# Hybrid decoder step: the product of the end-weighted x and B as three rounded products in units 2 to 5 of each group

## What is computed

```python
a_cum = jnp.cumsum(dtg * A.reshape(g, e).astype(f32), axis=2)
xdt = xg * dtg[..., None]
...
y_diag = jnp.einsum('bcijg,bcijge,bcjgep->bcigep', cb, decay, xdt)
decay_to_end = jnp.exp(a_cum[:, :, -1:] - a_cum)
chunk_states = jnp.einsum('bcjgn,bcjge,bcjgep->bcgepn', Bg, decay_to_end, xdt)
...
def step(s, inp):
    st, dec = inp
    return s * dec[..., None, None] + st, s
...
y_off = jnp.einsum('bcign,bcgepn,bcige->bcigep', Cg, starts, jnp.exp(a_cum))
```

## Time and profile before

| | us |
|---|---|
| median of 3 runs | 959.5 (958.59 to 961.35) |
| the profiled execution | 960.14 |
| its span | 958.3 |
| PE busy | 938.4 |
| DVE busy | 558.9 |
| ACT busy | 476.9 |
| POOL busy | 323.7 |
| PE, L1619, 20 products (40 records) | 587 to 692 ns a record, first at 544.3, last at 920.0 |

### The profile page before, as it was taken

How to read it: one execution, slowest core, us unless ns; L and a number is a source line. 1 busy time by engine, 2 the same in 40 slices (tenths; PEclk the granted TensorE clock), 3 DMA queues, 4 the chain that set the end, 5 groups by cost and what they waited for, 6 DMA issues and landing times.

```text
span 958.3 us, 18425 instructions
## 1 busy us (share of the span) xinstructions
PE 938.4 (98%) x7252; PEld 872.3 (91%) x7252; DVE 558.9 (58%) x1428; ACT 476.9 (50%) x943; POOL 323.7 (34%) x257
## 2 busy tenths in 40 slices
PE   9999999999999999999999999999999999999898
PEld 8998899989998899988998889998899989998787
DVE  4234421444225332447688679865898568986782
ACT  6335613365234623267537575446562565626852
POOL 2442244224431343224724232622434223442500
PEclk9999999999999999999999999999999999999999
DMA  7522231342143221211334825247152572327303
GB/s 212 181 75 68 77 100 53 110 152 77 57 118 146 95 88 52 89 23 45 113 96 128 233 61 168 89 119 222 46 162 91 151 205 70 128 85 216 108 12 105
DMA packets 144614, 105.91 MB, mean 111 GB/s; under 512 B 10754, under 2 KB 135860, under 8 KB 144464
## 3 DMA queue, kind: packets, MB, share of 16 engines
q1 hardware_dynamic: 134536, 100.19, 34.5%
q10 hardware_dynamic: 9992, 4.54, 2.0%
HBM read 91.99 MB, written 16.79 MB: 114 GB/s over the span
## 4 chain that ended last, share of the span: by engine, by line
PE 87%; DVE 9%; issue 2%; ACT 1%; DMA 0%; POOL 0%; SPq 0%; DVEq 0%; ACTq 0%; POOLq 0%
PE pp L1285 22%; PE pp L1287 21%; PE pp L1286 21%; PE pS L1395 2%; PE pO L1619 2%; PE pO L1615 2%; PE pT_ L1605 2%; PE pO L1442 1%; PE pO L1441 1%; DVE s_in L2312 1%; PE pO L1566 1%; PE pS L1538 1%; PE pp L1337 1%; PE pS L1576 1%; PE pT_ L1417 1%
## 5 line engine op out<-in xcount | busy, mean ns | idle before, releaser
L706 POOL TENSOR_TENSOR w_lo_buf<-w_raw_buf,w_hi_buf 128x512 fp32r<-128x512 f32 x214 | 278.9, 1334 | 475.7 <-ACT w_hi_buf L782 298.1
L1285 PE MATMUL pp<-h_hi,w_hi_buf 128*128 128x280 f32 (+2 forms) x1248 | 378.8, 304 | 2.1 <-issue 1.6
L1287 PE MATMUL pp<-h_hi,w_lo_buf 128*128 128x280 f32 (+2 forms) x1248 | 363.2, 291 | 0.0
L1286 PE MATMUL pp<-h_lo,w_hi_buf 128*128 128x280 f32 (+2 forms) x1248 | 362.6, 291 | 0.0
L1285 PEld LDWEIGHTS pp<-h_hi,w_hi_buf 128*128 128x128 f32 x1248 | 235.2, 188 | 11.9 <-issue 10.1
L1286 PEld LDWEIGHTS pp<-h_lo,w_hi_buf 128*128 128x128 f32 x1248 | 235.3, 189 | 5.3 <-issue 4.8
L1287 PEld LDWEIGHTS pp<-h_hi,w_lo_buf 128*128 128x128 f32 x1248 | 235.5, 189 | 0.0
L782 ACT ACTIVATE w_hi_buf<-w_raw_buf 128x2048 fp32r<-128x2048 f32 (+1 forms) x55 | 104.1, 1892 | 48.3 <-DMA w_raw_buf<-in_w_ssm_in 24.7
L1805 DVE TENSOR_TENSOR x<-x,pp 128x272 f32<-128x272 f32 (+2 forms) x120 | 53.1, 442 | 81.9 <-PE pp L1287 81.2
L1285 PE MATMUL pp<-og_hi,w_hi_buf 128*128 128x280 f32 (+2 forms) x256 | 75.6, 295 | 3.1 <-DVE x L1805 2.0
L1287 PE MATMUL pp<-og_hi,w_lo_buf 128*128 128x280 f32 (+2 forms) x256 | 74.5, 291 | 0.0
(11 more groups left out here) (357 smaller groups left out, 1613.8 us busy)
## 6 DMA issues: line engine op xcount, KB each, us to landing
w_raw_buf<-in_w_attn_in SPq DMA_DIRECT2D x16, 1024.0 KB, 5.2
w_raw_buf<-in_w_ssm_in SPq DMA_DIRECT2D x16, 1024.0 KB, 5.9
w_raw_buf<-in_w_attn_out SPq DMA_DIRECT2D x8, 1024.0 KB, 5.3
s_in<-in_state_ssm SPq DMA_DIRECT2D x32, 256.0 KB, 3.8
out<-s_in SPq DMA_DIRECT2D x32, 256.0 KB, 3.8
w_raw_buf<-in_w_ssm_out SPq DMA_DIRECT2D x8, 1024.0 KB, 6.6
seg<-a_scratch SPq DMA_DIRECT2D x12, 512.0 KB, 5.3
w_raw_buf<-in_w_attn_in SPq DMA_DIRECT2D x8, 512.0 KB, 6.2
```

Source lines behind the costliest of these rows:

```text
L706: ins = pool.tensor_tensor(low_buf(n)[:, piece], raw[n % RAW_SLOTS][:, piece], high_buf(n)[:, piece].bitcast(F32), ALU.subtract)
L1285: pe.matmul(dst, hi[:, k, cols], a_hi[:, k, tk], start=(k == 0), stop=False)
L1286: pe.matmul(dst, hi[:, k, cols], a_lo[:, k, tk], start=False, stop=False)
L1287: mm = pe.matmul(dst, lo[:, k, cols], a_hi[:, k, tk], start=False, stop=(k == depth - 1))
```

## The change

In units 2 to 5 of each group, 16 in all, the product of `btok` and `xw` is made of three products of rounded halves. The high half of B is a rounding copy from PSUM by DVE, the low half a DVE subtraction that waits for it; both stand in `prepare`. The high half of `xw` is a copy by ACT (`high_xw`, after `start_decay(u)`), its low half a subtraction by DVE in place of `xw` (`low_xw`, last in iteration u). The first of the three products waits for `low_xw`. `xw_hi` lies where `cv0` is, `btok_lo` where `sT1` is. Unit 1 (16 tokens) keeps its float32 product. Unit 0 has none.

```diff
--- before.py
+++ after.py
@@ -311,6 +311,9 @@
         xw = at("xw", [P, 2, WIDTH])
         cbm = at("cbm", [P, 2, P])
         btok = at("btok", [P, 2, P])
+        btok_hi = at("btok_hi", [P, 2, P], F32R, offset=where["btok"])
+        xw_lo = at("xw_lo", [P, 2, WIDTH], F32R, offset=where["xw"])
+        xw_hi = at("xw_hi", [P, 2, WIDTH], F32R, offset=where["cv0"])
         state = at("state", [P, WIDTH])
         ec = [at(f"ec{i}", [P, HEADS, P]) for i in range(2)]
         s_in = [at(f"s_in{i}", [P, HEADS, P]) for i in range(DEC_B - 2)]
@@ -318,6 +321,7 @@
         s_in += [at(f"s_in{6 + i}", [P, HEADS, P], offset=where["seg2"] + 4 * WIDTH * i) for i in range(2)]
         sT = [at(f"sT{i}", [P, WIDTH]) for i in range(2)]
         sT += [at("sT2", [P, WIDTH], offset=where["xdt"] + 4 * WIDTH), at("sT3", [P, WIDTH], offset=where["xw"] + 4 * WIDTH)]
+        btok_lo = at("btok_lo", [P, 2, P], F32R, offset=where["sT1"])
         c_own = at("c_own", [P, DEC_B * SAMPLE])
 
         x_parts = at("x_parts", [STACK, WIDTH], F32R, offset=where["rb0"] + 32)
@@ -369,6 +373,7 @@
         w_hi, w_lo = sem("w_hi"), sem("w_lo")
         p_done, p_evac = sem("p_done"), sem("p_evac")
         par_tr, par_ready, ones_ready = sem("par_tr"), sem("par_ready"), sem("ones_ready")
+        xw_high, xw_low = sem("xw_high"), sem("xw_low")
         x_tr, x_ready, h_ready = sem("x_tr"), sem("x_ready"), sem("h_ready")
         high_x = sem("high_x")
         sqx_ready, ssx_done, rs_ready = sem("sqx_ready"), sem("ssx_done"), sem("rs_ready")
@@ -1135,6 +1140,12 @@
                     act.wait_ge(clamped, w + 1)
                     act.activation(e, e, ACT.Exp, scale=-1.0).then_inc(l_done, 1)
 
+                def high_xw(u):
+                    v = UNITS * g + u
+                    act.wait_ge(xw_done, v + 1)
+                    act.wait_ge(b_done, v - 1)
+                    act.activation(xw_hi[:, v % 2, :], xw[:, v % 2, :], ACT.Copy).then_inc(xw_high, 1)
+
                 def start_decay(u):
                     act.wait_ge(ec_in[u % 2], 32 * (2 * g + (u - 2) // 2 + 1))
                     act.activation(ec[u % 2][:, :, :], ec[u % 2][:, :, :], ACT.Exp).then_inc(ec_ready, 1)
@@ -1184,6 +1195,7 @@
                         if u == 5:
                             start_decay(4)
                         start_decay(u)
+                    high_xw(u)
                     if (g, u) == (GROUPS - 1, 2):
                         silu_z(z_order(s)[0:HEADS])
                         exp_tables()
@@ -1616,7 +1628,15 @@
                                   start=True, stop=True)
                 if u == 1:
                     pe.wait_ge(sT_ready, DEC_B * (g + 1))
-                pe.matmul(pO[:, 0, :], btok[0:n, v % 2, :], xw[0:n, v % 2, :], start=True, stop=True).then_inc(b_done, 1)
+                if c == 0:
+                    pe.matmul(pO[:, 0, :], btok[0:n, v % 2, :], xw[0:n, v % 2, :],
+                              start=True, stop=True).then_inc(b_done, 1)
+                    return
+                pe.wait_ge(xw_low, 4 * g + u - 1)
+                pe.matmul(pO[:, 0, :], btok_hi[:, v % 2, :], xw_hi[:, v % 2, :], start=True, stop=False)
+                pe.matmul(pO[:, 0, :], btok_hi[:, v % 2, :], xw_lo[:, v % 2, :], start=False, stop=False)
+                pe.matmul(pO[:, 0, :], btok_lo[:, v % 2, :], xw_hi[:, v % 2, :],
+                          start=False, stop=True).then_inc(b_done, 1)
 
             def sum_y(g, part):
                 tk = part_of(g, part)
@@ -2105,11 +2125,22 @@
                     return
                 if c:
                     dve.tensor_tensor(cbm[0:n, b, 0:n], pS[0:n, 0, 0:n], mask, ALU.mult)
-                dve.tensor_copy(btok[0:n, b, :], pS[0:n, 0, P:2 * P])
+                if c:
+                    link(dve.tensor_copy(btok_hi[:, b, :], pS[:, 0, P:2 * P]))
+                    dve.tensor_tensor(btok_lo[:, b, :], pS[:, 0, P:2 * P], btok_hi[:, b, :].bitcast(F32), ALU.subtract)
+                else:
+                    dve.tensor_copy(btok[0:n, b, :], pS[0:n, 0, P:2 * P])
                 dve.tensor_tensor(heads(xdt[0:n, b, :], n), heads(pS[0:n, 1, :], n),
                                   per_head(tok2[0:n, 0, c, hs], n), ALU.mult)
                 dve.tensor_tensor(heads(xw[0:n, b, :], n), heads(pS[0:n, 1, :], n),
                                   per_head(wend[0:n, c, hs], n), ALU.mult).then_inc(xw_done, 1)
+
+            def low_xw(g, u):
+
+                v = UNITS * g + u
+                dve.wait_ge(xw_high, 4 * g + u - 1)
+                dve.tensor_tensor(xw_lo[:, v % 2, :], xw[:, v % 2, :], xw_hi[:, v % 2, :].bitcast(F32),
+                                  ALU.subtract).then_inc(xw_low, 1)
 
             def mix(g, u):
 
@@ -2331,6 +2362,7 @@
                         conv_in(g + 1, 0, u - 4)
                     if u > 2:
                         add_skip(g, u - 1)
+                    low_xw(g, u)
                 if g + 1 < GROUPS:
                     gate_y(g, 0)
                     conv_in(g + 1, 1, 0)
```

## The result

| | before | with the change |
|---|---|---|
| median, us | 959.4 (4 runs, 958.6 to 961.4) | 971.3 (4 runs, 969.7 to 972.3) |
| profiled execution, us | 960.1 | 969.7 |
| its span, us | 958.3 | 967.9 |

The ratio is 1.0126, 95% interval 1.0113 to 1.0140: slower by 11.9 us. Forecast were 7.2 slower, 966.7, with a range up to 970.5. The direction and the places of PE's waits were right, the size was not, and the result lies above the range.

What follows compares the result with a forecast made beforehand. PE was taken to bound the kernel. Groups 0 to 2 add 3.9 us and group 3 adds 3.3, +7.2 in sum: 967.3 for the profiled execution, 966.7 as median; range with the rivals 962.5 to 970.5.

Steps and rivals of the forecast that it cites:

- What bounds the kernel: PE, busy 938.4 of 958.3 us with 87% of the last chain; no gap in group 0's 6.76 us period.
- the ring: Groups 0 to 2: low_xw, PE's products, POOL's decay, DVE's row and back, 7.06 us a unit against PE's 6.58.
- DVE's uncovered row: Groups 0 to 2: DVE's gapless work from the state's addition to the next unit's first operation, 4.23 us, 5.06 in unit 4.
- The failed step: Unit 4, groups 0 to 2: low_xw takes 0.69 to 1.20 us beside POOL's split, making PE +1.2 to +1.7 us late.
- The 1.3 taken for a group: Loss chosen for each of groups 0 to 2 from a range of +1.0 to +1.5 us; three groups +3.9.
- PE's saving: Units 2 to 5: three rounded products take 0.68 us where one float32 product took 0.86; 16 x 0.18 = 2.9.
- Behind unit 5: End of groups 0 to 2: no cost added; unit 5's low_xw is in time and PE gets 0.18 us back.
- its own upper value: Groups 0 to 2: 1.5 us per group, which would hold if GpSimd contention slows low_xw as it did L2158.
- Group 3: ACT's late xw_hi delays mix(3) by 1.35 us; later waits make sum_y +3.3 us late.
- The one that cost more: Rival: products save nothing or low_xw takes 1.20 us everywhere in the nine binding products; +9 to +12 us, chance 0.14.
- Faster: Rival: all 16 waits fall inside earlier work and only PE's saving of 2.9 us is left; 956.6 us, chance 0.05.
- half covered: Rival: low_xw takes 0.3 us less, so the waits shrink; +4.5, 964 us; chance 0.09 for landing within 0.3%.

Runs made afterwards that it cites:

- e8: The change with POOL's splits of the weights in pieces of 256 columns instead of 512: 965.4 us, 6.9 above the kernel before.
- e5: The kernel before with DVE writing B and xw rounded and PE multiplying the high halves three times, no low halves: 956.8 us against 958.5.
- e4: The change's added DVE and ACT operations, but PE keeps the float32 product and waits for none of them: 964.4 us, 5.2 above the kernel before.
- e2: The change with ACT's xw_hi copy of unit 2 in group 3 moved behind the SiLU and table loads: 967.7 us, 8.6 above the kernel before.
- e7: As e4, without ACT's copy; DVE subtracts xw from itself and waits for no one: 962.1 us, 3.6 above the kernel before.
- e1: The change with low_xw moved right behind mix, ahead of the evacuation and add_skip: 969.5 us, 10.4 above the kernel before.
- e3: The change with POOL's weight split in groups 0 to 2 moved behind the state's decay of unit 4: 967.6 us, 8.4 above the kernel before.
- e9: The kernel before with POOL's splits in pieces of 256 columns instead of 512: 958.5 us against 958.4.
- e11: The change in groups 0 to 2 alone, group 3 computing as before: 967.1 us, 8.7 above the kernel before.
- e12: The kernel before with POOL pieces of 256 columns and the three rounded products only in unit 2 of groups 0 to 2: 958.0 us against 959.1.
- e10: The change with POOL pieces of 256 columns and ACT's copy of unit 2 in group 3 behind the SiLU: 963.6 us, 5.2 above the kernel before.

## Why the prediction was wrong

The trace puts the loss of groups 0 to 2 into few places. How much later than before the projection behind each product starts, counted from the start of part_a of unit 2 (from the starts of L1286 and L1298):

| us | unit 2 | unit 3 | unit 4 | unit 5 | whole group |
|---|---|---|---|---|---|
| forecast | -0.18 | +0.12 | +1.2 to +1.7 | +1.0 to +1.5 | +1.3 |
| group 0 | -0.16 | +0.23 | +2.49 | +2.32 | +2.57 |
| groups 1 and 2 | -0.16 | +0.23 | +2.50 | +2.32 | +2.28, +2.33 |

- *What bounds the kernel, and the ring.* Right. PE waits for `low_xw` in units 3 and 4 of groups 0 to 2 and not in units 2 and 5, POOL's decay and DVE's uncovered row being the way round. In unit 3 the first product starts just where it was forecast: 558.44 in the time of the kernel before, 556.83 plus the 1.61 by which this execution was ahead.
- *The failed step: unit 4, "`low_xw` 0.69 later if undisturbed, 1.20 if it is slowed as L2158 was".* It took 1.74. The bound above was the neighbour's stretch, read as a slowing down by 0.5. It was a wait for POOL's running piece: L2158 came when the third piece had 0.65 us left, `low_xw` when the fourth had 1.20 left, and both needed 0.55 more. A piece takes 1.3 us alone, so the bound should have been 1.3 + 0.6 = 1.9. e8 supports that: with pieces of 0.74 us it took 1.21, again 0.55 behind a piece's end. The 1.3 taken for a group stands for a `low_xw` of about 1.0 us, so this step was too small by about 0.75 a group, and the trace of the kernel before could have told.
- *PE's saving, 0.68 for three products.* Right where PE doesn't wait, 0.16 a unit. Behind a wait the three held PE 0.79 to 0.80, not 0.68, as the earlier start of 0.08 is lost. In units 3 and 4 that is 0.1 each. e5 shows 1.7 us in all, not 2.9, as part of group 3's saving falls into idle time, and a unit saves 0.16.
- *Behind unit 5.* The forecast put nothing there, and nearly nothing came: 0.26 in group 0, which is a longer wait of the output projection for `x` (0.46 against 0.17), and less than 0.05 in groups 1 and 2. The losses of e4 at this place appear when PE is not late itself.
- *The rule of the Trainium skill* (GPSIMD Engine Reference, "Key points", contention with VectorE instructions that have two SBUF inputs) pointed the right way: `low_xw` was held up, as was `mix` of unit 2 in group 3, while operations with an input in PSUM, such as L2186 (0.67 beside the second piece), were not. The trace agrees with the rule as to which operations are hit; the page gives no price. The forecast named its own upper value by the rule and then took less.
- *Group 3.* Forecast +3.3, measured +4.0 in the profile, and that it is so near is in part luck. The chain through ACT was right: `xw_hi` late by the SiLU, `mix` of unit 3 late, e2 gives 1.6 back in the stretch. But e8, with the same order of work, without the hold-up of `mix` of unit 2 and at full clock, loses only 2.4 there. So the forecast chain was worth about 0.9 less than stated, and two things it didn't have, that hold-up and the lower clock, made 1.6. How the 1.6 divides isn't shown; e4 and e7, at full clock, have the hold-up too (the product of unit 2 starts 1.05 and 0.79 later). From L1617 of unit 4 to that of unit 5 the change took 8.49 us (917.76 to 926.25), e2 at full clock 7.81 (916.09 to 923.90); the difference of 0.7 is an estimate of the clock's part, as e2's waits there differ too.
- *The rivals.* The one that cost more had the right sign of the error and the wrong reason: `low_xw` at 1.20 everywhere. It was slowed in one unit of four, but by twice as much. "Faster" and "half covered" were wrong. DVE's row was as long as the rows had shown, and `low_xw`, undisturbed, as long as its neighbour.
- *The range.* The sum with all its own upper values was +9, and it held no term for the clock. From the profile I had only full-clock slices in group 3 and so left it out.

By terms, then, for the three groups: 3 x 0.75 for the held-up subtraction, 3 x 0.27 for the products behind a wait and what they push back, 0.2 behind unit 5, and 0.7 for group 3 are 4.0; with 7.2 that is 11.2, the sum of the stretches.

## What to carry to other kernels

When an operation moves from one engine to two others, add up the path round through all of them once, with the time that each engine works without a gap. Here it came to 7.06 us where PE's own work took 6.58. Where the trace shows one VectorE operation stretched beside GpSimd, look at the single GpSimd instructions beside it: if it ends a fixed time behind one of them, it waited for it. Price the next operation of that form at GpSimd's whole running instruction plus its own time, and look for what else in the stretch is exposed to it, as `mix` of unit 2 in group 3 was, where a shift of a few tenths turned round who came first. And try the gain alone first: here e5 says 1.7 us before anything is paid.

## What the runs showed of the hardware

The hold-up is a wait for a turn, not a shared rate. A 128x512 VectorE subtraction or addition between SBUF tiles took 0.68 to 0.69 us alone. Where it met GpSimd's pieces of 512 columns it took 1.18 to 1.77, with pieces of 256 (median 740 ns each) 0.80 to 1.21. In the traces of the kernel before, the change, e1, e3, e4, e8 and e9 there are 36 of these long ones, and each ended 0.55 to 0.56 us behind the end of a GpSimd piece. GpSimd's pieces wait in the same way, from a median of 1293 ns to 2280 at most in the change.

The granted clock halves for some microseconds in stretches where PE had been partly idle, in some executions: in group 3 in the profiles of the change, e3, e9, e11 and e12, in group 1 in that of e11, and at about 512 us, ahead of the loop, in all four with pieces of 256 (e8, e9, e10 and e12) and in no other. One drop in group 1 of e11 cost 1.5 us. In e9, the executions with a mean clock of 0.997 to 1.0 took 955.4 to 957.8 us and those at 0.996 took 958.5 to 959.0, up to 3.5 us on the same program, of the size of what was to be measured. The four executions of the change lay at 0.994 to 0.998, those of before in the series of e1 to e4 at 0.998 to 0.999. So a part of the 11.9 us may be clock; by the price in e11 and the spread of e9 I estimate up to 2. But the change's own executions don't order by it (971.0 us at 0.998, 969.7 at 0.996). Whether the change makes the drop more frequent, or its place in time does, stays open: no run here forces it.
